# Prompt attention: in which tile the sample tokens' projection is computed

## The reference

```
xn = RMSNorm(x)
[a, b, q, k, v, g_A, g_B] = xn @ w_in
branch A: GLU(a, b) -> causal depthwise conv -> LayerNorm -> swish -> projection
branch B: sliding-window attention (window 128, 16 heads, 4 key heads, sinks, QK-norm, relative bias)
h = x + (sigmoid(g_A) * A + sigmoid(g_B) * B) @ w_out
y = h + HierMoE(RMSNorm(h))
```

## Time and profile before

| what | us |
|---|---|
| median of 3 runs | 1396.38 (1392.21 to 1398.14) |
| the profiled execution's own time | 1396.6 |
| its span | 1395.0 |
| PE busy | 1266.6 (91%) |
| DVE busy | 1089.0 (78%) |
| ACT busy | 711.7 (51%) |
| POOL busy | 278.2 (20%) |

### The profile page before, as it was taken

How to read it: one execution, slowest core, us unless ns; L and a number is a source line. 1 busy time by engine, 2 the same in 40 slices (tenths; PEclk the granted TensorE clock), 3 DMA queues, 4 the chain that set the end, 5 groups by cost and what they waited for, 6 DMA issues and landing times. The chain is left out here.

```text
span 1395.0 us, 23868 instructions
## 1 busy us (share of the span) xinstructions
PE 1266.6 (91%) x8743; PEld 762.6 (55%) x8743; DVE 1089.0 (78%) x1309; ACT 711.7 (51%) x1168; POOL 278.2 (20%) x279
## 2 busy tenths in 40 slices
PE   4889999967999999999999999989948999888875
PEld 2456666655666666666665666645524545443442
DVE  5678888885777999999995876536576999777783
ACT  4656656653344333542433554414125898666673
POOL 1282111110001100111000000000242576433322
PEclk9999999987799999999999999999978999999998
DMA  8700000032214423443241045475786999999962
GB/s 309 167 10 2 0 0 0 0 113 73 39 47 100 117 61 101 102 112 102 48 124 62 32 145 202 140 270 170 282 299 207 328 328 364 331 327 330 330 236 43
DMA packets 53068, 211.15 MB, mean 151 GB/s; under 512 B 14560, under 2 KB 15776, under 8 KB 40416
## 3 DMA queue, kind: packets, MB, share of 16 engines
q1 hardware_dynamic: 31888, 156.94, 31.2%
q0 software_dynamic: 18672, 44.42, 13.3%
q10 hardware_dynamic: 2448, 8.98, 1.6%
HBM read 180.97 MB, written 39.72 MB: 158 GB/s over the span
## 5 line engine op out<-in xcount | busy, mean ns | idle before, releaser
L1297 DVE SCALAR_TENSOR_TENSOR big<-c_region,c_taps,big 128x1024 f32<-128x1024 f32 (+1 forms) x120 | 153.4, 1278 | 3.7 <-ACT caT L997 3.7
L72 PE MATMUL c_psb<-xnT,w_taken 128*128 128x364 f16 x456 | 146.7, 322 | 2.3 <-DVE f_w_l L1192 2.3
L73 PE MATMUL c_psb<-xnT,w_taken 128*128 128x364 f16 x456 | 146.5, 321 | 0.0
L74 PE MATMUL c_psb<-xnT,f_w_l 128*128 128x364 f16 x456 | 146.3, 321 | 0.0
L1297 DVE SCALAR_TENSOR_TENSOR caT<-c_region,c_taps,caT 128x1024 f32<-128x1024 f32 x112 | 143.1, 1278 | 0.0
L72 PE MATMUL o_psH<-e_gu,big 128*128 128x512 f16 x256 | 100.2, 391 | 4.1 <-DVE big L2287 2.5
L74 PE MATMUL o_psH<-e_gu,big 128*128 128x512 f16 x256 | 100.1, 391 | 0.0
L73 PE MATMUL o_psH<-e_gu,big 128*128 128x512 f16 x256 | 100.0, 391 | 0.0
L72 PE MATMUL c_psa<-xnT,w_taken 128*128 128x364 f16 x312 | 99.1, 318 | 0.0
L74 PE MATMUL c_psa<-xnT,f_w_l 128*128 128x364 f16 x312 | 99.0, 317 | 0.0
L73 PE MATMUL c_psa<-xnT,w_taken 128*128 128x364 f16 x312 | 99.0, 317 | 0.0
(11 more groups left out here) (380 smaller groups left out, 3535.9 us busy)
## 6 DMA issues: line engine op xcount, KB each, us to landing
e_gu<-w_gu SPq DMA_DIRECT2D x34, 1024.0 KB, 20.3
w_taken<-w_feat SPq DMA_DIRECT2D x48, 512.0 KB, 3.7
e_d<-w_dn SPq DMA_DIRECT2D x17, 1024.0 KB, 23.3
xnT<-w_gu SPq DMA_DIRECT2D x14, 1024.0 KB
big<-w_gu SPq DMA_DIRECT2D x14, 1024.0 KB, 36.5
c_region<-gates POOLq DMA_DIRECT2D x8, 1092.0 KB, 5.7
xnT<-w_dn SPq DMA_DIRECT2D x7, 1024.0 KB
big<-w_dn SPq DMA_DIRECT2D x7, 1024.0 KB
```

The source lines that it names most:

```text
L72: pe.matmul(out, stat[0], mov[0], start=start, stop=False)
L73: pe.matmul(out, stat[0], mov[1], start=False, stop=False)
L74: return pe.matmul(out, stat[1], mov[0], start=False, stop=stop)
L1297: dve.scalar_tensor_tensor(y_j, glu[:, p, j:j + SEQ], tap, y_j, op0=ALU.mult, op1=ALU.add).then_inc(tap_done, 1)
```

## The change

The six half pieces of tile 8, their three copies, the squares and the mean squares move from tile 6 into tile 7. Tile 6 then has none: it is taken out of the loops of PE and ACT and written by itself (`ahead=False`). Tile 7 gets them at places of its own (`last=True`). On PE two halves stand after `scores` 1, one after `turn_p` 0, and three in a row after `scores` 3. On ACT the copies stand after `exps` 0, 1 and 2, the squares behind the third. On DVE `mean_squares` stands directly ahead of `norms`, and tile 7 is taken out of the loop. The other engines' code is as it was.

```diff
@@ ACT
-                if not last:
+                if ahead:
                     piece(t + 2, 0)
+                if last:
+                    piece(NT, 0)
                 turned_p(t, 0, first)
                 exps(t, 1, lo)
+                if last:
+                    piece(NT, 1)
                 turned_p(t, 1, first)
                 exps(t, 2, lo)
-                if not last:
+                if ahead:
                     piece(t + 2, 1)
+                if last:
+                    piece(NT, 2)
+                    squares(NT)
                 turned_p(t, 2, first)
...
-            with act.Fori(1, NT - 1) as t:
+            with act.Fori(1, NT - 2) as t:
                 tile(t)
-            tile(NT - 1, last=True)
+            tile(NT - 2, ahead=False)
+            tile(NT - 1, ahead=False, last=True)
@@ DVE
-                mean_squares(t + 1)
+                if not last:
+                    mean_squares(t + 1)
                 logits(t, 0, lo)
...
                 low_p(2)
+                if last:
+                    mean_squares(t + 1)
                 norms(t + 1)
@@ PE
                 scores(t, 1, first)
-                if not last:
+                if ahead:
                     half_piece(t + 2, 0, 1)
+                if last:
+                    half_piece(NT, 0, 0)
+                    half_piece(NT, 0, 1)
                 scores(t, 2, first)
                 turn_p(t, 0, first)
-                if not last:
+                if ahead:
                     half_piece(t + 2, 1, 0)
+                if last:
+                    half_piece(NT, 1, 0)
                 values(t, 0, first)
                 turn_p(t, 1, first)
                 scores(t, 3, first)
-                if not last:
+                if ahead:
                     half_piece(t + 2, 1, 1)
+                if last:
+                    half_piece(NT, 1, 1)
+                    half_piece(NT, 2, 0)
+                    half_piece(NT, 2, 1)
                 turn_p(t, 2, first)
                 values(t, 1, first)
```

More of the change, by code:

```diff
@@ L392, in turned_p, with tile @@
                 act.activation(pT_h[:, grp % 2, 0:n], psT[:, 0:n], ACT.Copy, scale=S_X).then_inc(T_high, 1)
-            def tile(t, first=False, last=False):
+            def tile(t, first=False, ahead=True, last=False):
                 lo = P if first else 0
@@ L553, in _, with tile @@
             dve.memset(g.oT_l[:, :, T:TP], 0.0).then_inc(setup_done, 1)
-            def tile(t, first):
+            def tile(t, first, last=False):
                 lo = P if first else 0
@@ L588, in _ @@
             tile(0, True)
-            with dve.Fori(1, NT) as t:
+            with dve.Fori(1, NT - 1) as t:
                 tile(t, False)
+            tile(NT - 1, False, True)
             low_turned(g.oT_l[:, :, (NT - 1) * P:NT * P], g.oT_h[:, :, (NT - 1) * P:NT * P], use_q(NT))
@@ L753, in _ @@
             tile(0, first=True)
-            with pe.Fori(1, NT - 1) as t:
+            with pe.Fori(1, NT - 2) as t:
                 tile(t)
-            tile(NT - 1, last=True)
+            tile(NT - 2, ahead=False)
+            tile(NT - 1, ahead=False, last=True)
             pe.wait_ge(T_free, use_q(NT))
```

## The result

The changed kernel took 1414.54 us (median of 4 runs, 1409.89 to 1422.29) against 1396.56 us before; the ratio is 1.0141, 95% interval 1.0105 to 1.0176. It is slower by 18 us, inside the forecast range (1403 to 1420) and 2.5 us above the forecast sum of 1412. Built once more and timed with 6 runs, it took 1412.83 us, ratio 1.0130 (1.0111 to 1.0149).

What follows compares the result with a forecast made beforehand. VectorE's chain was taken to bound the attention phase, which a barrier ends. Tile 6 +1.6, tile 7 +12.3 and clock +1.8 gave +15.7 us on 1396.6: 1412, range 1403 to 1420.

Steps and rivals of the forecast that it cites:

- Tile 6, +1.6: Tile 6 without its pieces becomes as tile 7 was, with TensorE's clock falling: +1.6 us, bounds 0 and +3.2.
- The 0.55 us of earlier start: Start of tile 7: without squares on ScalarE ahead of its q split, its chain may start 0.55 us earlier.
- The walk through tile 7: Tile 7 with the pieces, step by step at full clock: last output at 46.2 instead of 33.9, +12.3 us.
- Step 4: Tile 7: ScalarE waits from 19.8 to 25.0 for the second piece, with transposed group 1 ready at 21.0; VectorE waits too.
- step 5: Tile 7: third piece done at 30.9, transpose 2 ends at 32.0; ScalarE's third copy and squares delay group 2's copy to 34.2.
- The first rival: Pieces in tile 7 fill gaps and hold the clock, tile 6 loses nothing: about 1393 us, chance 0.04.
- Step 6, the round to the root: Tile 7: VectorE stands still for the root until 40.7, norms end at 43.3, last output at 46.2.
- The second rival: Only the round to the root enters VectorE's chain, +4.0, and +1.6 for tile 6: about 1402 us, chance 0.12.
- The clock: Tile 7 starts behind an idle stretch, so its first matmuls may run at 1.2 GHz: +1.8 us, bounds 0 and +8.5.
- the third rival: The clock stays low through tile 7's dense part, +8.5 in place of +1.8: about 1419 us, chance 0.14.
- Hidden: Five next-phase loads land at about 43 in tile 7, ahead of the last output at 46.2: 0, up to 3 us.
- the straight code that was priced at 0: One more tile written as straight code on each engine was taken to cost 0.

Runs made afterwards that it cites:

- no_pieces: Changed kernel without the sample tokens' projection, copies, squares, root and norms, so tiles 6 and 7 have no pieces; 1396.11 us, ratio 0.9997 to the kernel before.
- fill_six: Changed kernel plus six groups of 12 matmuls with unused results in tile 6, where its half pieces stood; 1410.10 us, ratio 1.0104 to the kernel before.
- norms_last: Changed kernel with tile 7's norms on VectorE moved behind the fourth output; 1407.00 us, ratio 1.0086 to the kernel before.
- act_order: Changed kernel with ScalarE's copy of the second piece in tile 7 moved behind the copy of transposed group 1; 1414.05 us, ratio 1.0140 to the kernel before.
- spread: Changed kernel, tile 7: last two half pieces behind values 1, ScalarE's piece copies later, mean squares before and norms behind the fourth output; 1406.14 us, ratio 1.0077 to before.
- norms_only: Kernel before with only the sample tokens' norms in tile 7 moved behind the fourth output; 1396.56 us, ratio 1.0006.
- warm_seven: Kernel before plus six groups of 12 matmuls with unused results in tile 7 and one group behind the last transposes; 1394.94 us, ratio 1.0000.

## Why the prediction was right, and where its reasons were not

- **What bounds it.** A tile can lose its pieces without getting shorter: shown by no_pieces (tile 6 34.16 against 31.97). That VectorE stands still in tile 6 only at both ends was not quite so: its timeline has waits of 0.43, 0.57 and 0.42 us inside.
- **Tile 6, +1.6.** Measured 33.88 against 31.97, +1.9, and 2.0 to 2.3 in the others. That it is the clock is shown by fill_six (2.6 us back).
- **The 0.55 us of earlier start.** It did not come: the q transposes ran at the half clock (1.95 us against 1.07) and the split began 3.1 after the tile (289.82 - 286.69) instead of 2.8 before (288.05 - 285.27). In norms_last and fill_six, where they ran at the full clock, it began at 2.3, the 0.5 earlier that was forecast.
- **The walk through tile 7.** It was right to 0.1 us in this execution (48.0 forecast with the clock, 47.98 measured) and 0.9 too long in its repetition (47.06), so the tenth is luck. The clock cost at its start about what I had charged. Forecast at the full clock and measured: first half piece 9.0 and 10.7, scores 2 14.2 and 15.9, fourth half piece 22.3 and 23.8, third transposes 30.9 and 32.4, output 3 43.3 and 44.5, output 4 46.2 and 48.0. The lag is 1.7 at the first half piece, 1.2 at output 3 and 1.8 at the end; the clock was priced at 1.8. The last 0.6 arose between outputs 3 and 4, which lie 3.45 apart instead of 2.89.
- **Step 4, "the costly place".** Wrong as a cause, though not in the sum: act_order took ScalarE's wait (5.08 us in the row, 5.2 forecast) away for nothing. The chain went over step 5, TensorE's three half pieces and, behind them, ScalarE's third copy and squares; spread shows it, with output 4 5.5 us earlier. The 4.8 us by which spread's output 4 is still later than before (38.76 against 33.92) no run divides. With this falls what I wrote of the first rival, that it is decided by when group 1 is copied: in act_order the copy began 22.6 after the tile, against 27.1, and the time stood. The first rival itself fell: tile 7 lost 14 us instead of getting 1.6 back, and tile 6 lost 1.9.
- **Step 6, the round to the root.** Idle 3.64, forecast 3.5 (40.7 less 37.2). Shown by norms_last, with 3.0 to 3.6 us of the phase. The second rival, that this round alone counts, fell with it: in norms_last the phase is still 12.9 us longer than before, 2.1 of them tile 6's.
- **The clock.** The size was about right. The reason given, an idle stretch in tile 6 ahead, does not carry it: with tile 6 at full clock (fill_six) the first half piece began no earlier. The clock was low in tile 7's own start, which has no half piece, and was up by the time the first two ran (means of 0.61 from 292 to 296, 0.96 from 296 to 300, 1.00 from 300 to 304). So the third rival fell. The rule of the Trainium skill ("TensorE: Matmul & The Clock Gate", section "Why this matters for your kernels") that a continuously busy TensorE gets its full clock back agrees with this stretch, as it did not with 372 to 376 us of the kernel before. The first two of these stretches:

```profile
292.00:296.00 4.00, 2.94 (x29) 2.73 (x28) 1.16 (x3) 1.02 (x1) 0.00 (x0) 0.61 0.00 0
296.00:300.00 4.00, 4.00 (x37) 2.59 (x35) 3.82 (x5) 1.21 (x5) 0.00 (x0) 0.96 0.01 4
```

- **Hidden.** The loads were, by 4 us (330.7 against 334.67), and TensorE's first matmuls on the next phase's weights began 4.6 us after the phase's end in both kernels.
- **The sum.** The phase lost 16.4 by the table (15.9 in the repetition) and 15.7 was forecast. The 16.4 are 1.9 of tile 6, 14.1 of tile 7 and 0.45 of the tail behind output 4 (6.48 against 6.03 us; its transposes ran wholly at the half clock), which the forecast had left as it was. The median moved 18.0 in one set and 18.1 in the other. Of the difference 0.8 us lies outside the span (2.4 against 1.6 in the profiled executions; medians of all runs 2.7 and 2.5 in the two sets, against 1.6). It is also higher, 2.0, in norms_only, whose only other difference is one tile more written straight on VectorE, so the straight code that was priced at 0 may be its cause; no run tests that. What is left, some 1 us, lies in the stretch behind the phase, which the forecast held constant and which varied by 4.5 us between two executions of the same kernel; whether the change has a part in it is not shown.

## What to carry to other kernels

Matmuls that no one waits for are filler only where TensorE would wait anyway. Before moving them, walk the chain of the new place: three in a row ahead of a transpose cost their length, and a result needed within the same tile brings its whole round (copy, squares, root, norms) with it. A long wait of one engine in the profile need not cost anything; ask what runs beside it, and take it away before calling it the cause: ScalarE's 5.08 us went and nothing moved.

## What was not expected of the hardware

Tile 6 got 1.9 to 2.3 us longer for losing 15.5 us of TensorE's work, since the granted clock fell to 0.50 in parts of it; twelve-matmul groups without use gave more than that back (31.31 us in tile 6 of fill_six, and 31.59 in tile 7 of warm_seven against 33.92 before). And a shorter phase by 2.7 us did not show in the time of the whole program, in two sets of runs; 1.0 us of it went into a slower issue of one load at the start of the next phase.
